# Two fp32r weight tiles and eight activation tiles get other start addresses in SBUF

## The reference

```python
# first block
u_lat = modulate(x, sh1, sc1) @ w_in                    # 1024 -> 2064, also for 256 context tokens
x = post_norm(x, mixer(u_lat) @ w_out, ...)
a = dwconv2d_grid(modulate(x, sh2, sc2) @ w_up, ...)    # 1024 -> 2 x 2816
x = post_norm(x, (gelu(gate) * val) @ w_down, ...)      # 2816 -> 1024
# second block, two layers
proj = rms_norm(h) @ w_in                               # 1024 -> 2640
h = h + concatenate([attention, mlstm]) @ w_out
h = h + square(relu(rms_norm(h) @ w_ff1)) @ w_ff2       # 1024 -> 4096 -> 1024
h = h + sigmoid(rms_norm(h) @ w_ple_gate + b) * (p @ w_ple)
```

## Time and profile before

| what | value |
|---|---|
| median of three runs | 2059.4 us |
| span of the profiled execution | 2057.3 us |
| PE busy | 2013.4 us (98%) |
| PE weight loads busy (beside the matmuls) | 1574.5 us (77%) |
| DVE, ACT, POOL busy | 1135.5, 867.9, 917.4 us |
| chain that ended last | PE 88%, DVE 6%, POOL 2%, ACT 2% |
| DMA | 94 GB/s, 28.5% of 16 engines for the queue of the weights |

### The profile page before, as it was taken

How to read it: one execution, slowest core, us unless ns; L and a number is a source line. 1 busy time by engine, 2 the same in 40 slices (tenths; PEclk the granted TensorE clock), 3 DMA queues, 4 the chain that set the end, 5 groups by cost and what they waited for, 6 DMA issues and landing times.

```text
span 2057.3 us, 26250 instructions
## 1 busy us (share of the span) xinstructions
PE 2013.4 (98%) x10148; PEld 1574.5 (77%) x10148; DVE 1135.5 (55%) x2020; ACT 867.9 (42%) x1381; POOL 917.4 (45%) x1157
## 2 busy tenths in 40 slices
PE   6999999999999999999999999999999999999998
PEld 2877676888888767768888888786776788888877
DVE  5366758988393579955522231466996543222235
ACT  4542434443233556784322222445578532222242
POOL 1344205876566325541555555302355155555540
PEclk9999999999999999999999999999999999999999
DMA  9034631322323211103333323322111332332331
GB/s 328 25 108 143 217 123 50 105 94 80 121 84 102 89 42 42 62 21 123 92 103 103 99 86 103 102 69 83 42 42 42 103 97 98 103 103 83 102 102 62
DMA packets 188299, 194.26 MB, mean 94 GB/s; under 512 B 8592, under 2 KB 184080, under 8 KB 187792
## 3 DMA queue, kind: packets, MB, share of 16 engines
q1 hardware_dynamic: 187600, 189.44, 28.5%
q10 hardware_dynamic: 576, 3.15, 0.4%
HBM read 190.48 MB, written 2.10 MB: 94 GB/s over the span
## 4 chain that ended last, share of the span: by engine, by line
PE 88%; DVE 6%; POOL 2%; ACT 2%; DMA 1%; issue 1%; SPq 0%; DVEq 0%; ACTq 0%; POOLq 0%
PE ps L808 20%; PE ps L810 20%; PE ps L809 20%; PE ps L827 3%; PE ps L829 3%; PE ps L828 3%; PE ps L855 2%; POOL wl L2900 1%; DVE mix L2512 1%; PE ps L844 1%; PE ps L845 1%; PE ps L846 1%; PE ps L1355 1%; PE ps L1428 1%; PE ps L1411 1%; PE ps L1374 1%
## 5 line engine op out<-in xcount | busy, mean ns | idle before, releaser
L2900 POOL TENSOR_TENSOR wl<-ring,wh 128x256 fp32r<-128x256 f32 x1008 | 754.2, 783 | 807.5 <-ACT wh L1465 807.2
L1465 ACT ACTIVATE wh<-ring 128x1024 fp32r<-128x1024 f32 (+1 forms) x298 | 309.0, 1044 | 311.1 <-PE ps L810 256.9
L808 PE MATMUL ps<-xh,wh 128*128 128x512 f32 (+1 forms) x976 | 383.1, 393 | 2.6 <-POOL wl L2900 2.6
L810 PE MATMUL ps<-xh,wl 128*128 128x512 f32 (+1 forms) x976 | 380.6, 390 | 0.0
L809 PE MATMUL ps<-xl,wh 128*128 128x512 f32 (+1 forms) x976 | 380.6, 390 | 0.0
L808 PE MATMUL ps<-acts,wh 128*128 128x512 f32 x880 | 343.5, 390 | 0.7 <-POOL wl L2900 0.4
L810 PE MATMUL ps<-acts,wl 128*128 128x512 f32 x880 | 342.4, 389 | 0.0
L809 PE MATMUL ps<-acts,wh 128*128 128x512 f32 x880 | 342.4, 389 | 0.0
L2512 DVE SCALAR_TENSOR_TENSOR mix<-ps,par,mix 128x441 f32<-128x441 f32 (+2 forms) x352 | 213.7, 687 | 29.3 <-ACT mix L1712 29.3
L808 PEld LDWEIGHTS ps<-xh,wh 128*128 128x128 f32 (+1 forms) x976 | 183.0, 188 | 47.0 <-issue 9.1
L810 PEld LDWEIGHTS ps<-xh,wl 128*128 128x128 f32 (+1 forms) x976 | 183.0, 187 | 39.4
(11 more groups left out here) (443 smaller groups left out, 3031.4 us busy)
## 6 DMA issues: line engine op xcount, KB each, us to landing
ring<-in_w_ff_dram SPq DMA_DIRECT2D x64, 1024.0 KB, 5.2
ring<-in_w_in_dram SPq DMA_DIRECT2D x28, 1024.0 KB, 5.0
ring<-in_ffn_w_up_dram SPq DMA_DIRECT2D x22, 1024.0 KB, 4.9
ring<-in_w_ada_dram SPq DMA_DIRECT2D x17, 1024.0 KB, 5.0
ring<-in_w_out_dram SPq DMA_DIRECT2D x12, 1024.0 KB, 5.1
ring<-in_ffn_w_down_dram SPq DMA_DIRECT2D x8, 1024.0 KB, 5.0
ring<-in_w_ple_gate_dram SPq DMA_DIRECT2D x8, 1024.0 KB, 5.0
early<-in_w_ada_dram SPq DMA_DIRECT2D x7, 1024.0 KB, 10.8
```

The costliest lines, as they stand in the source:

```text
L808: t.matmul(b[0:m, 0:n], s.hi[:, k, a:a + m], x2[0][:, k, :], start=k == ks[0], stop=False)
L810: i = t.matmul(b[0:m, 0:n], s.lo[:, k, a:a + m], x2[0][:, k, :], start=False, stop=k == ks[-1])
L1465: a.activation(s.hi[:, :, c], s.ap[:, :, c], ACT.Copy).then_inc(*up("hi", "hi", name, hf))
L2900: i = p.tensor_tensor(s.lo[:, k:k + 2, c], s.ap[:, k:k + 2, c], s.hi[:, k:k + 2, c].bitcast(F32), ALU.subtract)
```

## The change

The split-weight tiles `wh` and `wl` are asked for before `turn`, `h`, `xh` and `xl` instead of after them. The tiles of inner activations become a little wider, and each hi and lo half starts at an offset of its own. No instruction, wait or transfer is added, removed or moved in any engine's list.

```diff
         rope, eps, csil_t, small = sb("rope", 64), sb("eps", 3), sb("csil", 256), sb("small", 1024)
+        wh_t, wl_t = sb("wh", 2 * SLOT, F32R), sb("wl", 2 * SLOT, F32R)
         turn_t = sb("turn", 108)
         h_t, xh_t, xl_t = sb("h", 4096), sb("xh", 4096, F32R), sb("xl", 4096, F32R)
-        wh_t, wl_t = sb("wh", 2 * SLOT, F32R), sb("wl", 2 * SLOT, F32R)
         mix_t, ring = sb("mix", 4096), sb("ring", NSLOT * SLOT)
...
-            acts = sb("acts", 16384, F32R, where=low)
-            U1 = [[acts[:, (2 * u + v) * 4096:(2 * u + v + 1) * 4096].rearrange("p (j t) -> p j t", j=8)
-                   for v in range(2)] for u in range(2)]
+            acts = sb("acts", 16896, F32R, where=low)
+            U1 = [[acts[:, o:o + 4096].rearrange("p (j t) -> p j t", j=8) for o in two] for two in ((112, 4320), (8528, 12736))]
...
-                a0 = sb(f"acts{l}0", 8192, F32R, where=low)
+                a0 = sb(f"acts{l}0", 8320, F32R, where=low)
                 with ExitStack() as high:
-                    a1 = sb(f"acts{l}1", 8192, F32R, where=high)
+                    a1 = sb(f"acts{l}1", 8448, F32R, where=high)
...
-            n.U = [[a[:, v * 4096:(v + 1) * 4096].rearrange("p (j t) -> p j t", j=8) for v in range(2)] for a in (a0, a1)]
+            n.U = [[a[:, o:o + 4096].rearrange("p (j t) -> p j t", j=8) for o in two]
+                   for a, two in zip((a0, a1), (((8, 4216), (104, 4228)), ((12, 4144), (32, 4184)))[l])]
```

## The result

The changed kernel takes 2091.8 us in the median of four runs (2089.2 to 2094.82), against 2059.23 us for the kernel before beside it. The ratio is 1.0159, with a 95% interval of 1.0145 to 1.0173: slower by 32.6 us, where 14.9 us less were forecast and the range ended at 2062 us. The profiled execution spans 2087.4 us, 30.1 us more than before.

A forecast was written before the change was run, and what follows sets the result against it. The prediction took PE's matmul count times the distance of starts to bound the kernel. Gains of 8.0 + 5.9 + 1.0 = 14.9 us from 2059.4 gave 2044.5 us, range 2020 to 2062 us.

The forecast's parts named there:

- What bounds the kernel: PE, busy 98% of the span: time is the number of matmuls times the distance between their starts, 226.7 ns at 512 columns.
- Step (a): Matmuls moving `xh` or `xl` over 512 columns, weights shifted to 64: 2.1 ns gained each, 8.0 us in all.
- The end on the losing side: For matmuls moving `xh` or `xl`: 5.3 ns more each, 20 us lost, from the slowest cadence seen, 232 ns.
- Step (b): Matmuls moving the inner activations at new distances from the weights: 2.1 ns gained each, 5.9 us in all.
- The prediction's own sign against (b): Inner activation tiles differing among each other by over 3 ns would mean distance matters finely and their gain was mis-sized.
- Step (c): Matmuls where weights move over stationary `xh` or `xl`, distance +64: half of 2.1 ns gained each, 1.0 us.
- Step (d): Matmuls moving `ctxr`, distance from the weights going from 448 to 384: 0, give or take 0.3 us.
- Step (e): Other engines and transfers using the moved tiles: costed at nothing; PE's whole wait for the split was 5.4 us.
- My reading of the fixed part: The 13 ns per matmul beyond its columns' time is two SBUF reads costing each other, partly set by start addresses.
- the cost mostly goes: New distances end the meeting of two reads: 2035 or 2020 us, 1977 us if everywhere; chance 0.20 (under 2036 us).
- the inner activations get slower: In the two layers, 2304 matmuls lose 5.3 ns each, 12.2 us in all: 2061.5 us; chance 0.12 (over 2063 us).
- second form: Layers' inner activations lose 5.3 ns a matmul and the gain for `xh` and `xl` fails too: 2071 us; chance 0.12 (over 2063).

The follow-up runs named there:

- widths experiment: Streams-only kernel, computation left out, 512 to 128 columns moving, 128 to 32 stationary, differences 0 to 192 bytes: with 512 moving, 226.7 ns (128 stationary), 231.7 (32).
- three maps of this shape: Streams-only kernels, 512 columns moving, varying starts of moving tiles against weights, of moving hi and lo, of weight hi and lo: least 226.7 ns.

## Why the prediction was wrong

*What bounds the kernel* was right: PE in streams, time equal to the count times the distance of starts. The account above closes within 2 us on it. The granted clock stayed as it was in sum (26 steps at the lower level's distance before and after, some at other times), and so did the other engines and the transfers.

*Step (a)* failed, in sign. It took the gain of `ctxr`, 2.1 ns at a difference of -64 with 256 columns moving, for the price of the same difference with 512 columns. The reason given was that the fixed part is 13 ns at both widths. That was shown for the difference 0 alone. The widths experiment has it side by side: at 0 the fixed part is 13.3 ns for 512 and for 256 columns, at 192 (which is -64) it is 20.0 and 6.7. The step came out at 5.9 ns lost instead of 2.1 gained (6.6 in undisturbed streams), 21.5 us for 8.0 us. The end on the losing side, 5.3 ns from the earlier trace rows, was nearly the size, but it had no weight in the sum, since those rows have another cause.

*Step (b)* failed with it: 4.7 ns lost for 2.1 gained, 13.1 us. It had the right warning, that no row showed any of its distances (there are twelve), and then used the nearest of two. One row at another width is no bound for a function whose form isn't known; here it jumps by 6.6 ns in one step of 16 bytes. The prediction's own sign against (b) came out, tiles that differ by more than 3 ns: 228.9 to 233.3 ns. And its distances, taken modulo 512, hid that the one of 256 is the same as 0.

*Step (c)* was right in sign and too small: 3.1 ns gained, 2.7 us for 1.0. The sign was in part luck, since no row had its distance; with 256 columns moving 0 happens to be nearly the dearest start. *Step (d)* held, 0.8 ns lost where a change within 1 ns was foretold. *Step (e)* held: PE's waits for the split are 4.6 us in sum, 5.4 before.

*My reading of the fixed part*, two reads that cost each other, was half right. Relative starts matter, which the `ctxr` row had shown truly, and the Trainium skill's rule in "SBUF — State Buffer", section "SBUF: two separate sides", that PE never waits on anyone on the engine side, doesn't cover what was measured here: 226.7 and 233.3 ns by start addresses alone. But a cost that follows the size of what is read is not there, and for the rival *the cost mostly goes*, which had 0.20, nothing was found: 226.7 ns is the least in three maps of this shape. The 215.8 ns worked out from the Trainium skill's "TensorE: Matmul & The Clock Gate", section "Back-to-back issue gap", whose formula is for an isolated matmul, was reached by no fp32r stream of 512 columns with a weight load for every matmul. The fp32 records' 2.4 ns stand at half the rate and were no floor for full rate.

*The rival that came true* was *the inner activations get slower* in its second form, with (a) failing too, at 2071 us. It had 0.12 and was too small as well, since it let `xh` and `xl` lose nothing. The rows of before allowed as well that 0 was the best start for 512 columns: of 6624 matmuls none was elsewhere, so the trace had no row for or against it, and a loss deserved a chance no smaller than a gain.

## What to carry to other kernels

Where two operands of a stream of matmuls are moved against each other in memory, the distance of starts can change: with the hi and lo tiles alike it went up from equal starts by up to 3.5% with 512 columns moving, and down by up to 5.5% with 256. A value read at one width says nothing of another. Before such an edit, measure the pairs in a small kernel of streams with the very shape and order of the real one: 256 pairs fit in 1.5 ms of chip time. They show what no arithmetic could here, though a stream can take another value in the real kernel, where other streams come before it. For fp32r with 128 stationary and 512 moving columns, equal starts modulo 256 bytes are as good as any here, and tiles whose sizes are multiples of 256 bytes keep them so without further thought.

## What was not expected of the hardware

- The distance of starts depends on moving start minus stationary start modulo 256 bytes: 226.7 to 234.6 ns with 512 columns moving, 113.3 to 120.0 ns with 256, and up to 242.3 ns where the hi and lo tiles start apart. Moving all tiles together by 32 bytes, or one side by 256, leaves it alone.
- The extra over the columns' own time prefers 6.7, 13.3 and 20.0 ns (16, 32 and 48 cycles), and with 512 columns moving it is larger with 32 stationary columns (18.4 ns) than with 128 (13.3 ns).
- Streams have more than one steady state at the same addresses: 113.3 and 117.8 ns at 192, 226.7 and 236.6 ns at 240, and in the changed kernel itself 231.1 and 233.3 ns. The maps differ in what ran before.
- The clock fell to its lower level for about 3 us in places where the profiled execution of the kernel before, with the same instructions, kept the full one: twice in the kernel with all tiles moved (3.1 us lost), once in the one with the mixers' input at 64 (1.6 us). It differs between executions of one kernel too: 2066.2 us at a mean clock of 0.993, 2058.0 on average at 0.998. For differences of 1 to 3 us in 2059 the granted clock has to be read first.
- Transfers of 1 MB from HBM to starts at 480 instead of 0 modulo 512 landed in 12.1 instead of 10.8 us at the beginning, and in 5.4 instead of 5.2 or 5.3 us in the ring.
